# Split-operand linear layers of a two-block transformer kernel, with one ring of 1 MB weight tiles

## The reference

```python
for layer in range(2):
    h = h + hybrid_mixer(rmsnorm(h, norm_mix_g[layer]), ...)
    h = h + memory_cross_attention(rmsnorm(h, norm_x_g[layer]),
                                   rmsnorm(mem, norm_mem_g[layer]), w_xq, w_xkv, w_xo)
    hn = rmsnorm(h, norm_ffn_g[layer])
    h = h + (swiglu(hn, ...) if layer % 2 == 0 else moe_swiglu(hn, ...))   # 2816 wide | 8 experts, top 2

def hybrid_mixer(xn, w_in, ...):
    a_val, a_gate, b_gate, c_gate, b_in, c_z = split(xn @ w_in)      # 384, 384, 320, 320, 320, 640
    ya = silu(layernorm(causal_conv31(a_val * sigmoid(a_gate)) + bias))
    yb = b_gate * causal_conv3(c_gate * b_in)
    c_u, c_v = split(gelu(c_z))
    yc = c_u * (masked 128x128 spatial mix of layernorm(c_v))
    return rmsnorm_by_64(concat(ya, yb, yc)) @ w_mix_out

def memory_cross_attention(xn, memn, w_xq, w_xkv, w_xo):              # 4 heads of 256, 256 memory rows
    q = xn @ w_xq;  k, v = split(memn @ w_xkv)
    return softmax(q k^T / 16) v @ w_xo
```

## Time and profile before

| | |
|---|---|
| median of 3 runs | 2892.71 us (2880.12 to 2893.2) |
| the profiled execution | 2884.54 us, span 2882.8 us |
| busy: PE, DVE, ACT, POOL | 92%, 65%, 38%, 9% of the span |
| layer 0 mixer and attention | 14 to 287 us |
| layer 0 feed-forward | 294 to 484 us |
| layer 1 mixer and attention | 491 to 762 us |
| routing and experts | 762 to 1811 us |
| second block up to PEER, PEER | 1811 to 2188 us, 2188 to 2883 us |

### The profile page before, as it was taken

How to read it: one execution, slowest core, us unless ns; L and a number is a source line. 1 busy time by engine, 2 the same in 40 slices (tenths; PEclk the granted TensorE clock), 3 DMA queues, 4 the chain that set the end, 5 groups by cost and what they waited for, 6 DMA issues and landing times.

```text
span 2882.8 us, 31202 instructions
## 1 busy us (share of the span) xinstructions
PE 2665.8 (92%) x11607; PEld 2037.1 (71%) x11607; DVE 1879.1 (65%) x2828; ACT 1084.4 (38%) x1140; POOL 247.0 (9%) x280
## 2 busy tenths in 40 slices
PE   9999999999899999999999999799999897877877
PEld 7768999867778888888888888688788453332332
DVE  5331653631388888897888888246523887888775
ACT  1212332021267768677776866121601111110110
POOL 0000000000000000000000000000001344333331
PEclk9999999999899999999999999799999999899999
DMA  6331654521289999999899998442254999999997
GB/s 236 117 117 44 205 182 150 185 88 59 102 307 334 373 333 357 347 352 350 332 372 333 358 347 294 148 146 74 105 190 154 399 421 421 422 421 422 421 421 320
DMA packets 277347, 775.18 MB, mean 269 GB/s; under 512 B 12661, under 2 KB 52735, under 8 KB 244223
## 3 DMA queue, kind: packets, MB, share of 16 engines
q1 hardware_dynamic: 239648, 503.41, 48.6%
q0 software_dynamic: 36864, 268.45, 22.5%
q10 hardware_dynamic: 735, 1.99, 0.2%
HBM read 772.76 MB, written 1.05 MB: 268 GB/s over the span
## 4 chain that ended last, share of the span: by engine, by line
PE 77%; DMA 14%; DVE 5%; issue 2%; ACT 1%; POOL 0%; DVEq 0%; ACTq 0%; POOLq 0%
DMA dense_weights<-in_peer_rows,work 14%; PE banks L692 13%; PE banks L694 13%; PE banks L693 13%; PE banks L531 13%; PE banks L581 5%; PE banks L1069 3%; PE banks L547 2%; PE banks L655 2%; PE banks L659 2%; PE banks L492 2%; PE banks L1031 1%; PE banks L849 1%; PE banks L778 1%; PE banks L805 1%
## 5 line engine op out<-in xcount | busy, mean ns | idle before, releaser
L1967 DVE TENSOR_TENSOR expert_tiles_low<-expert_tiles,expert_tiles_high 128x2048 fp32r<-128x2048 f32 x336 | 752.9, 2286 | 89.8 <-ACT expert_tiles_high L1485 89.6
L1485 ACT ACTIVATE expert_tiles_high<-expert_tiles 128x2048 fp32r<-128x2048 f32 x336 | 624.8, 1912 | 65.6 <-DMA expert_tiles<-in_moe_w_down 52.6
L1069 PE MATMUL banks<-dense_weights,work 128*128 128x512 f32 x952 | 457.7, 633 | 115.7 <-DVE work L2299 115.5
L1069 PEld LDWEIGHTS banks<-dense_weights,work 128*128 128x128 f32 x952 | 186.0, 201 | 376.2 <-issue 208.9
L692 PE MATMUL banks<-expert_tiles_high,gathered_parts 128*128 128x512 f32 x896 | 355.4, 397 | 2.2 <-DVE gathered_parts L1976 2.2
L694 PE MATMUL banks<-expert_tiles_high,gathered_parts 128*128 128x512 f32 x896 | 350.5, 391 | 0.0
L693 PE MATMUL banks<-expert_tiles_low,gathered_parts 128*128 128x512 f32 x896 | 349.9, 391 | 0.0
L2289 DVE CUSTOM_DVE_ANT_0 dense_weights<-dense_weights,banks 128x1024 f32<-128x1024 f32 x238 | 286.2, 1218 | 85.2 <-DMA dense_weights<-in_peer_rows,work 83.4
L1292 POOL DMA_INDIRECT dense_weights<-in_peer_rows,work x238 | 223.7, 940 | 731.1 <-DVE work L2258 372.4
L1674 ACT ACTIVATE work<-work 128x2 f32<-128x2 f32 x129 | 26.2, 203 | 558.9 <-DVE work L2289 555.6
L692 PEld LDWEIGHTS banks<-expert_tiles_high,gathered_parts 128*128 128x128 f32 x896 | 169.0, 189 | 36.3 <-issue 2.4
(11 more groups left out here) (364 smaller groups left out, 3670.1 us busy)
## 6 DMA issues: line engine op xcount, KB each, us to landing
expert_tiles<-in_moe_w_gate SPq DMA_DIRECT2D x112, 1024.0 KB, 5.1
expert_tiles<-in_moe_w_up SPq DMA_DIRECT2D x112, 1024.0 KB, 5.1
expert_tiles<-in_moe_w_down SPq DMA_DIRECT2D x112, 1024.0 KB, 4.8
dense_weights<-in_w_in SPq DMA_DIRECT2D x12, 2048.0 KB, 9.6
dense_weights<-in_w_xkv SPq DMA_DIRECT2D x8, 2048.0 KB, 7.9
dense_weights<-in_w_in SPq DMA_DIRECT2D x10, 1280.0 KB, 13.9
expert_tiles<-in_ffn_w_gate SPq DMA_DIRECT2D x11, 1024.0 KB, 5.1
expert_tiles<-in_ffn_w_up SPq DMA_DIRECT2D x11, 1024.0 KB, 5.2
```

The lines of the kernel that those rows point to most:

```text
L1069: mm = pe.matmul(halves[half], diag[(first + j) % 8], pair_row(first + j)[:, 1, half * 512:(half + 1) * 512], start=False, stop=end and j ...
L1485: act.activation(high_tile(j), raw_tile(j), ACT.Copy).then_inc(g.high, 1)
L1967: dve.tensor_tensor(low_tile(j), raw_tile(j), high_tile(j).bitcast(F32), ALU.subtract).then_inc(g.split, 1)
```

## The change

- Both layers' mixer, attention and feed-forward go through `split_tile` and `split_group`: three products of high and low parts, each 128x128 by 256 columns. `parts` stays for the feed-forward's second half and the experts.
- There is one ring of 7 raw tiles of at most 1 MB for everything outside the experts, with 3 high tiles. Tiles are at most 256 columns wide; a section of the mixer is two tiles (256 columns, and 128 or 64).
- ScalarE writes every high tile. `round_until` does it inside `ready(key)`: before ScalarE waits for a group, it has rounded the tiles up to two beyond the one that the group uses. A high slot is written again when the tile three before it has been used.
- GpSimd computes every low tile (`low_part`), for all 101 split tiles, in order. For layer 0's feed-forward this was VectorE's work.
- ScalarE rounds `x`, `y` and `o` per k; VectorE computes their low parts (`split_x`), and `mem_high` and `mem_low`.
- In the mixer, `memory()`, `mem_g` and its two parts stand before the convolution on VectorE, and the memory's sum of squares before c_gate on PE.
- Loads of the memory are issued by ScalarE behind the rounding of x. The group norm's `std8` and `o`'s banks are at other places. PEER's row buffers are other slots, and the last four join at rows 20, 36, 52 and 68 instead of 36, 37, 68 and 69.

```diff
-RING = 5
-EXP_RING = 7
-SLOT_F = KT * 512
+RING = 7
+HIGH_RING = 3
+TILE_F = KT * 256
-BUF_JOINS = {11: 2 * TOPK + 4, 12: 2 * TOPK + 5, 13: 4 * TOPK + 4, 14: 4 * TOPK + 5}
+BUF_JOINS = {11 + i: (i + 1) * TOPK + 4 for i in range(4)}
...
+            def split_group(bank, tile, widths, high_x, low_x):
+                high, low = tile
+                for k in range(KT):
+                    for i, m in enumerate(widths):
+                        o, n_ = bank[0:m, i * SEQ:(i + 1) * SEQ], slice(i * P, i * P + m)
+                        pe.matmul(o, high[:, k, n_], high_x(k), start=(k == 0 and i == 0), stop=False)
+                        pe.matmul(o, low[:, k, n_], high_x(k), start=False, stop=False)
+                for k in range(KT):
+                    for i, m in enumerate(widths):
+                        mm = pe.matmul(bank[0:m, i * SEQ:(i + 1) * SEQ], high[:, k, i * P:i * P + m], low_x(k),
+                                       start=False, stop=(k == KT - 1 and i == len(widths) - 1))
+                return mm
...
+                section("a_gate", "a", P)
+                section("a_val", "v", P)
                 if l == 0:
                     norm_sums("mem_ms", 1)
+                section("c_gate", "a", 64)
...
+            def low_part(j):                                    # GpSimd
+                n, size = G.splits[j], G.sizes[j]
+                pool.wait_ge(tiles_rounded, j + 1)
+                pool.tensor_tensor(low_tiles[:, n % RING, 0:size], raw_tiles[:, n % RING, 0:size],
+                                   high_tiles[:, j % HIGH_RING, 0:size].bitcast(F32), ALU.subtract).then_inc(tiles_split, 1)
+            for j in range(len(G.splits)):
+                low_part(j)
...
+            def round_until(count):                             # ScalarE
+                nonlocal rounded
+                while rounded < min(count, len(G.splits)):
+                    j, n, size = rounded, G.splits[rounded], G.sizes[rounded]
+                    if j >= HIGH_RING:
+                        act.wait_ge(*G.freed[G.splits[j - HIGH_RING]])
+                    act.wait_ge(loads[n % RING], G.need[n])
+                    act.activation(high_tiles[:, j % HIGH_RING, 0:size], raw_tiles[:, n % RING, 0:size], ACT.Copy).then_inc(tiles_rounded, 1)
+                    rounded += 1
+            def round_ahead(key):
+                round_until(G.splits_at[key] + AHEAD)
             def ready(key):
+                round_ahead(key)
                 act.wait_ge(group_done, G.after[key])
...
-                key_value(5, 6, 7)
+                key_value(5)
+                for k in range(KT):
+                    act.wait_ge(y_ready, KT * l + k + 1)
+                    act.activation(x_high[:, k, :], yF[:, k, :], ACT.Copy).then_inc(y_rounded, 1)
+                key_value(6, 7)
...
+                if l == 0:                                      # VectorE, before conv(conv_a, ...)
+                    memory()
+                dve.wait_ge(mem_normed, 1)
+                for k in range(KT):
+                    step.then(dve.tensor_scalar(mem_g[:, k, :], mem_hat[:, k, :], c_vec(l, MEM_G, k), None, ALU.mult))
+                step.settle()
+                step.now(dve.tensor_copy(mem_high, mem_g))
+                dve.tensor_tensor(mem_low, mem_g, mem_high.bitcast(F32), ALU.subtract).then_inc(mem_ready, 1)
```

More of the change, by code:

```diff
@@ L79 @@
 FFN_TILES = FFN_GATE_UP + FFN_DOWN
-FFN_HIGH = 3
 WARM = 13
@@ L554, in weight @@
-            def weight(slot, kts, widths, cols_n=None):
-                n = cols_n or 512
-                return ring[:, slot, 0:kts * n].rearrange("p (k n) -> p k n", k=kts)
+                    w = weight(G.plain_tile())
+                    bank = G.begin(who, (key, tile))
+                    for i in range(2):
+                        for k in range(KT):
+                            mm = pe.matmul(bank[:, i * SEQ:(i + 1) * SEQ], w[:, k, i * P:(i + 1) * P], x(k),
+                                           start=(k == 0), stop=(k == KT - 1))
@@ L559, in _, with split_linear @@
+            def split_linear(key, who, x, dmas=1):
+                for g in range(4):
+                    tile = split_tile(KT, 2 * P, dmas)
+                    bank = G.begin(who, (key, g))
+                    G.end(split_group(bank, tile, (P, P), *x))
+                    G.free()
             pe.wait_ge(ones_ready, 1)
@@ L571, in mixer, with section @@
                     norm_sums(("mix_ms", l))
[L572 to L588 removed]
+                x = normed_split()
+                def section(name, who, last):
+                    for g, widths in enumerate(((P, P), (last,))):
+                        tile = split_tile(KT, sum(widths))
+                        bank = G.begin(who, (name, l, g))
+                        G.end(split_group(bank, tile, widths, *x))
+                        G.free()
+                section("a_gate", "a", P)
+                section("a_val", "v", P)
                 if l == 0:
                     norm_sums("mem_ms", 1)
[L591 to L594 removed]
+                section("c_gate", "a", 64)
+                section("b_in", "v", 64)
+                section("b_gate", "a", 64)
+                section("c_v", "a", 64)
+                section("c_u", "a", P)
                 def three(src):
@@ new lines, in y_low_part @@
+                def y_low_part(k):
+                    pe.wait_ge(y_split, KT * l + k + 1)
+                    return y_low[:, k, :]
+                split_linear(("mix_out", l), "v", (y_high, y_low_part), dmas=4)
+            def key_value(l, i):
+                high, low = tile = split_tile(KT, 2 * P)
+                bank = G.begin("a", ("kv", l, i))
+                if i < 4:
+                    mm = split_group(bank, tile, (P, P), lambda k: mem_high[:, k, :], lambda k: mem_low[:, k, :])
+                else:
+                    for b in range(TB):
+                        s, o = slice(b * P, (b + 1) * P), bank[:, b * SEQ:(b + 1) * SEQ]
+                        for k in range(KT):
+                            pe.matmul(o, mem_high[:, k, s], high[:, k, :], start=(k == 0), stop=False)
+                            pe.matmul(o, mem_high[:, k, s], low[:, k, :], start=False, stop=False)
+                            mm = pe.matmul(o, mem_low[:, k, s], high[:, k, :], start=False, stop=(k == KT - 1))
@@ L1421, in attention @@
             def attention(l):
-                norm(("x_ms", l), G.took[("mix_out", l), 3])
+                norm(("x_ms", l), ("mix_out", l))
+                round_x()
                 copies(("q", l), qF)
@@ L1785, in wide @@
                     return ap.unsqueeze(1).to_broadcast([P, n, SEQ])
-                if l == 0:
-                    memory()
-                dve.wait_ge(mem_normed, 1)
-                for k in range(KT):
-                    ins = dve.tensor_scalar(mem_g[:, k, :], mem_hat[:, k, :], c_vec(l, MEM_G, k), None, ALU.mult)
-                    if k < KT - 1:
-                        step.then(ins)
-                ins.then_inc(mem_ready, 1)
                 dve.wait_ge(act_took, G.took["c_mean", l])
@@ new lines, in feed_forward @@
+                split_x()
+                for c in range(FFN_GATE_UP // 2):
+                    ready(("ffn", 1, c))
+                    dve.wait_ge(act_took, G.took["ffn", 0, c])
+                    h, s = hid[:, c % 2, :, :], slice(2 * c, 2 * c + 2)
+                    take(dve.tensor_tensor(h, pair(bank_of(("ffn", 1, c))), sil[:, c % 2, :, :], ALU.mult))
+                    dve.wait_ge(dve_took, G.took["ffn", 1, c])
+                    step.now(dve.tensor_copy(hid_high[:, s, :], h))
+                    dve.tensor_tensor(hid_low[:, s, :], h, hid_high[:, s, :].bitcast(F32), ALU.subtract).then_inc(ffn_hid_split, 1)
```

402 lines of the change are left out of this document (169 added, 233 removed).

## The result

The changed kernel took 2912.3 us (median of five runs, 2909.8 to 2916.5) against 2885.6 for the kernel before (five runs, 2877.2 to 2893.2), a ratio of 1.0095 with a 95% interval of 1.0066 to 1.0123. The predicted 2905 is 7 us too low; the forecast of the sign (slower, 0.43) and the serialised case hold. As a change, though, the sum had +11 against the profiled execution, and the spans say +27.8 (2882.8 to 2910.6). That the two totals lie so close is in part luck: the forecast had 8 us added for the median of the first three runs before the change (2892.7), and the median of all five came out at 2885.6. The steps behind it have to be looked at one by one.

The account below looks back on a forecast made before the run. PE was taken to bound the changed part, with little slack on VectorE. Layer 0 at +8 and layer 1 at +3 gave 2884.5 + 11 = 2896, and 8 us for median over profiled execution gave 2905; range 2842 to 2930.

Parts of the forecast that it names:

- the sign: Whole kernel: slower 0.43, same 0.28, faster 0.29, with half a percent (14 us) as the threshold.
- the serialised case: Mixer's convolution: VectorE's two-input steps and GpSimd's subtractions wait for each other; +11 us in all, chance 0.42.
- PE's pace: Split products on PE: three cost 0.36 us instead of 0.434, a full tile 5.8 instead of 6.9.
- the products are no cheaper: Rival on PE: the three split products save no time over the plain one; no chance of its own given.
- The conflict: Mixer's convolution: GpSimd's subtractions, 4.1 us a full tile, add 24.8 us a layer to VectorE's two-input steps.
- The start of layer 0: First section of layer 0's mixer: PE starts near 17.5 us instead of 13.95, behind tile 0's remainder.
- mix_out's wait: Before mix_out: its first tile is rounded behind y, so PE idles 6 us and runs slowly after; +2.0 us a layer.
- Behind layer 1: Second block and PEER: products, buffers and transfers stay as they are; 0, between -3 and +3 us.
- No conflict: Rival in the convolution: VectorE and GpSimd read side by side at full pace; -48 us, median 2845, chance 0.18.
- Starves: Rival in the convolution: GpSimd gets no turn until VectorE's steps end; +29 us, median 2922, chance 0.17.
- POOL is the bound: Rival for split tiles: GpSimd's subtraction at 6.2 us is slower than PE's 5.8; about +65 us, chance 0.07.
- Shared: Rival in the convolution: VectorE and GpSimd slow each other, half of 24.8 us added; some -16, median 2877, chance 0.12.

Follow-up runs that it names:

- experiment 2: The changed kernel with GpSimd's subtraction replaced by two multiplications of the tile by zero, one SBUF input each: 3275.5 us, ratio 1.1354.
- experiment 1: The changed kernel with GpSimd's subtraction of a tile replaced by two memsets of the same tile, which write but don't read: 2846.8 us, ratio 0.9862.
- experiment 4: The changed kernel with the memory's norm, gains and two parts put back behind the convolution and b branch on VectorE, both layers: 2926.4 us, ratio 1.0141.
- Experiment 3: The changed kernel with ScalarE's first wait a plain one that no longer rounds two weight tiles before the squares of x: 2910.5 us, ratio 1.0083.
- Experiments 5 and 7: 5: the changed kernel with mix_out's first tile rounded ahead of y, 2909.1 us; 7: the same plus the mixer's seven sections as single fp32 products, 2848.7 us.

## Why the prediction came out as it did

The working had layer 0 at +8, layer 1 at +3, the rest at 0, between -3 and +3. Measured by the landmarks: layer 0 with its feed-forward +21.6, layer 1 +12.2, the rest -6.0, which lies outside the range given for it.

- **PE's pace: right.** In the feed-forward a tile takes 5.76 us (the third product of two tiles in a row, on the chain, at 321.61 and 327.37), a product 0.120 us; mix_out's tiles 5.72 and xo's 5.65. x_ms to ffn_ms shrank from 82.4 to 73.8 us in layer 0. The rival "the products are no cheaper" is out. The same pace saves nothing in the sections, since VectorE sets that stretch.
- **The conflict: right in kind, too small in size.** I took 5 x 4.1 + 2.1 + 2.2 = 24.8 us from the start of the convolution on. (The prediction names b_in among the sections that are left and PE in c_gate, but five full tiles are the count without b_in; with it they are six and three of 64, 30 us by the same price.) VectorE's stretch is 10.7 in `mem_g`, 5.3 in the three first taps and 15.2 in the 90 steps, 31.2 us; in layer 1 it is 31.3 (the cast 4.3, the low part 1.0, 5.3 and 20.7). Two terms were mis-sized. I charged only what falls beside the two-input steps, but the one-input `mem_g`, cast and first taps were held up as well. And GpSimd's subtraction is dearer than 4.1:

```profile
L1303 POOL TENSOR_TENSOR weight_tiles_low<-weight_tiles,weight_tiles_high 128x2048 fp32r<-128x2048 f32 (+2 forms) x101 | 435.5, 4321 | 342.3 <-ACT weight_tiles_high L1346 342.3
```

  That mean mixes shapes; the 87 full tiles take 4.71 on average, most of them 4.55 to 4.85 (two that began beside a VectorE instruction of 2.29 us with two inputs took 6.69 and 5.76). Nor do the runs bear out the way to 4.1, two reads one after the other at 2.1 us each: in experiment 2 a multiplication of a full tile, with one read, took 5.4 us. That 4.1 came as near as it did is luck. The Trainium skill (GPSIMD Engine Reference, Performance versus the Vector engine) has 4.497, and its price would have been the better one to take: a sum of +17. Of the other page (SBUF — State Buffer, Who interferes with whom) experiment 1 shows the rule in both halves for two-input steps: 50.94 us beside a GpSimd that reads, 35.74 beside one that only writes. The same section says that whoever issues first has the ports for the whole instruction. The traces agree for the single instruction: a step lasts 4.84 us beside a subtraction of 4.84. For a whole queue of steps experiment 4 shows both outcomes: GpSimd was kept out for 31.9 us of back-to-back steps in one layer, and took its turns in the other.
- **The start of layer 0: wrong, and the failed step.** "PE starts near 17.5": it starts at 24.20. I had ScalarE round tile 0 while x is normed, and overlooked that the very first wait in its queue is a `ready`, which rounds two tiles before the squares and so waits for a load that lands at 11.15. With the 6.7 us of this and the 6.4 of the stretch, the variance of c_v ends at 135.2 where 122.4 was predicted; the two terms, 13.1 together, account for the 12.8. In layer 1, which has no such start, the variance came 16.1 us later within its layer where 11.1 was predicted; the longer stretch (31.3 instead of 24.8) more than covers the 5.0. Experiment 3 shows that the wait alone isn't worth 6.7, since the earlier norm of x meets GpSimd.
- **Between the variance and a_mean: about right.** +3.5 predicted (idle PE starts slow, rounding of group 2), +4.6 measured (21.4 to 26.0), with the granted clock at 0.59 from 125 to 161 us, that is mostly at 1.2 GHz after 34.85 us without work.
- **mix_out's wait: right.** 48.8 us from a_mean predicted, 49.9 measured, PE idle 7.36 (6 predicted). Experiments 5 and 7 show that it hangs on one place in ScalarE's order: a_mean to x_ms falls by 6 to 9 us when the tile is rounded ahead.
- **The rest of a layer: nearly right.** a_mean to x_ms: mix_out -4.8, the wait +2.0 and the norm of y +1.5 give -1.3; measured -1.2 and -1.7. x_ms to the next norm: -10.2 for q, xo and `o`; measured -8.6 and -6.4. ffn_ms to mix_ms: -3 predicted, -5.2 measured.
- **Behind layer 1: 0 within 3 predicted, -6.0 measured.** Of this -3.8 is the second block's start, from the experts' last sums to norm1 (19.5 to 15.7 us), where PE had an "issue" wait of 2.77 us between the sums before and has none after the change; 1.1 each lie in the experts and between norm1 and norm2. No run isolates any of them.
- **The rivals.** "No conflict" is out by the 50.94 us, and experiment 1 gives its time, 2847, near the 2845 worked out. "Starves" did not happen in the changed kernel and did in layer 0 of experiment 4. "POOL is the bound" needs over 5.8 us a tile: experiment 2 has nearly 11 and pays 363 us for it. "Shared" is out: 0.89 of GpSimd's time is added, not half, and it falls on single steps that wait a whole subtraction out.

So the expected gain did arrive from a_mean on: 14.9 us in layer 0 with its feed-forward and 8.2 in layer 1. It was overdrawn by the sections, where split products save PE time that PE didn't lack: the convolution on VectorE sets that stretch, and the remainders that the split needs were put on an engine whose reads shut VectorE out. With plain sections and one tile rounded earlier the same change gives 1.3%.

## What to carry to other kernels

Work moved to an idle GpSimd is not free while VectorE is near the path: here each GpSimd instruction that read SBUF held one VectorE instruction for nearly its whole length, 0.89 of GpSimd's time in sum, so ask first which stretch VectorE sets, and keep GpSimd's reads out of it. Split a product only in stretches where TensorE is late. And follow each engine's queue from its very first wait: a helper that prefetches in front of a wait moved the first sums of the kernel by 7 us, and one whose turn came behind eight other instructions left PE idle for another 7 in each layer.

## What the runs showed of the hardware that was not expected

- While GpSimd subtracts, one VectorE instruction waits for the whole of it: a convolution step took 4.84 us instead of 0.47.
- VectorE's one-input steps are held up by a reading GpSimd as well: eight of them took 12.93 us instead of 2.19. A GpSimd that only writes stretched them to 4.11 us and left two-input steps alone.
- GpSimd's one-input multiplication of a 128x2048 fp32 tile into fp32r takes 5.4 us, longer than its two-input subtraction of the same tile (4.6); its memset takes 1.8.
- Back-to-back VectorE steps kept GpSimd out for 31.9 us, so that one subtraction lasted 36.24 us, or let it in ten times, in the two layers of one kernel (experiment 4).
